# Dilated attention with its tokens tiled by parity: four blocks of 128 keys in every step of a two-layer decoder kernel

## What is computed

```
B_GROUPS = ((128, 1), (512, 4), (2048, 16))     # (window, dilation)
...
# Query t attends keys t, t-dil, ..., t-win (causal)
s = q . k * dh ** -0.5 + bias[bucket(distance)]
...
w = softmax over the groups of their lse
out = sum over the groups of w * o
```

## Time and profile before

| | |
|---|---|
| median of 3 runs | 798.08 us (796.19 to 800.15) |
| the profiled execution | 795.02 us, of which 793.0 us are the span |
| TensorE clock granted | 0.993 of full speed |
| TensorE busy | 97% of the span |
| VectorE, ScalarE, GpSimd busy | 68%, 58%, 29% |
| the attention blocks | 65.2 us each, from about 324 to 585 us |

### The profile page before, as it was taken

The page is one execution under the profiler, slowest core; times in us unless marked ns, Lnnn a source line. Parts: engine busy times, 40 slices in busy tenths (PEclk is TensorE's granted clock), DMA queues, the critical chain, the costliest instruction groups (busy, mean ns, idle before and its releaser), DMA issues.

```text
span 793.0 us, 17171 instructions
## 1 busy us (share of the span) xinstructions
PE 767.4 (97%) x6550; PEld 751.1 (95%) x6550; DVE 538.5 (68%) x983; ACT 462.4 (58%) x608; POOL 226.7 (29%) x190
## 2 busy tenths in 40 slices
PE   7999989999999999999999999999999999999995
PEld 7989889999999999999999999999899999999995
DVE  5776867887888546557646646655678888788442
ACT  6642657666565456358647737735856665655451
POOL 2520224333222532222222221201232234222331
PEclk9999999999999999999999999999999999999998
DMA  9653425665655555856586295475625756554721
GB/s 292 205 160 110 150 80 193 212 197 175 199 188 183 182 184 176 241 175 145 173 237 141 84 258 122 148 218 157 168 70 188 238 173 199 176 195 147 239 93 53
DMA packets 135613, 137.27 MB, mean 173 GB/s; under 512 B 3521, under 2 KB 134932, under 8 KB 135572
## 3 DMA queue, kind: packets, MB, share of 16 engines
q1 hardware_dynamic: 127808, 130.03, 50.4%
q10 hardware_dynamic: 7764, 6.67, 6.6%
HBM read 135.57 MB, written 1.12 MB: 172 GB/s over the span
## 4 chain that ended last, share of the span: by engine, by line
PE 53%; DVE 24%; issue 11%; ACT 7%; DMA 2%; DVEq 1%; ACTq 0%; POOL 0%; POOLq 0%
DVE wlo L845 9%; PE bank L1301 7%; PE bank L1303 6%; PE bank L1302 6%; PE banks L1301 6%; PE banks L1303 6%; PE banks L1302 6%; DVE cb L1090 3%; PE bank L1523 3%; PE banks L1590 2%; PE bank L1525 2%; DVE bank L1084 2%; ACT cb L671 2%; PE bank L1524 2%; PE banks L1555 2%
## 5 line engine op out<-in xcount | busy, mean ns | idle before, releaser
L453 POOL TENSOR_TENSOR wlo<-raw,whi 128x512 fp32r<-128x512 f32 (+1 forms) x169 | 218.2, 1324 | 530.4 <-ACT whi L494 530.4
L494 ACT ACTIVATE whi<-raw 128x2048 fp32r<-128x2048 f32 (+1 forms) x136 | 238.0, 1751 | 198.0 <-PE banks L1303 81.0
L845 DVE TENSOR_TENSOR wlo<-raw,whi 128x1024 fp32r<-128x1024 f32 x161 | 197.9, 1267 | 15.8 <-ACT whi L494 15.1
L1301 PE MATMUL bank<-xsA,whi 128*128 128x256 f32 x568 | 159.5, 281 | 3.6 <-DVE wlo L920 3.4
L1303 PE MATMUL bank<-xsA,wlo 128*128 128x256 f32 x568 | 157.7, 278 | 0.0
L1302 PE MATMUL bank<-xsA,whi 128*128 128x256 f32 x568 | 157.7, 278 | 0.0
L1301 PE MATMUL bank<-xsB,whi 128*128 128x256 f32 x480 | 134.3, 280 | 0.4 <-DVE cb L1094 0.3
L1303 PE MATMUL bank<-xsB,wlo 128*128 128x256 f32 x480 | 132.7, 276 | 0.0
L1302 PE MATMUL bank<-xsB,whi 128*128 128x256 f32 x480 | 132.6, 276 | 0.0
L1301 PEld LDWEIGHTS bank<-xsA,whi 128*128 128x128 f32 x568 | 107.4, 189 | 5.1 <-issue 4.1
L1302 PEld LDWEIGHTS bank<-xsA,whi 128*128 128x128 f32 x568 | 107.5, 189 | 0.1
(11 more groups left out here) (209 smaller groups left out, 1577.4 us busy)
## 6 DMA issues: line engine op xcount, KB each, us to landing
raw<-in_f_w_up SPq DMA_DIRECT2D x44, 1024.0 KB, 5.1
raw<-in_w_kv SPq DMA_DIRECT2D x24, 1024.0 KB, 7.6
raw<-in_f_w_down SPq DMA_DIRECT2D x16, 1024.0 KB, 5.2
raw<-in_b_w_q SPq DMA_DIRECT2D x12, 1024.0 KB, 5.3
raw<-in_a_w_in SPq DMA_DIRECT2D x10, 1024.0 KB, 5.8
raw<-in_f_w_down SPq DMA_DIRECT2D x8, 768.0 KB, 4.9
Bi<-bias_by_distance ACTq DMA_DIRECT2D x16, 384.0 KB, 7.7
raw<-in_a_w_out SPq DMA_DIRECT2D x4, 1024.0 KB, 5.2
```

Source lines behind the costliest of these rows:

```text
L453: o = g.tensor_tensor(wlo[s][:, ka:kb, :], raw[s][:, ka * CW:kb * CW] .rearrange("p (k c) -> p k c", c=CW), whi[s][:, ka:kb, :].bitcast(F3 ...
L494: o = a.activation(whi[s][:, k0:k1, :], raw[s][:, k0 * CW:k1 * CW] .rearrange("p (k c) -> p k c", c=CW), ACT.Copy)
L845: v.tensor_tensor(wlo[s][:, ka:kb, :], raw[s][:, ka * CW:kb * CW].rearrange("p (k c) -> p k c", c=CW), whi[s][:, ka:kb, :].bitcast(F32), A ...
L1301: t_.matmul(ps, hi_w, hi_x, start=first, stop=False)
```

## The change

Tokens go into two tiles by parity, the even ones and the odd ones. A group with dilation 4 or 16 then needs only the key tile of the query's own parity, and the group with dilation 1 needs both. Each step has four blocks of 128 keys: 512 wide, exactly one PSUM bank. The order of the tokens is changed where the input of the attention is made (`gained`, by `by_parity`, on ScalarE and VectorE in the last stage of layer 0) and changed back where a head's output is stored (`head_out`). The bias table has 5 rows of 256 for a head: group 0 for same parity, groups 1 and 2, and group 0 for the other parity twice, for the two directions. Scores rotate over banks 3 to 5, transposes alternate between banks 6 and 7.

```
-DIST = 384
+DIST = 512
+BB = 5
...
-    dist = 255 - np.arange(DIST)
+    m = np.arange(DIST // 2)
+    dist = np.concatenate([254 - 2 * m, 255 - 2 * m])
...
         def score_out(s):
-            w = NG * P * (1 + s // 2 % 2)
-            c = s % 2 * (768 if s // 2 % 2 else 512)
-            return s_ps[:, c:c + w]
+            return bank[3 + s % 3][:, :]
+        def turned_bank(s):
+            return bank[6 + s % 2][:, :]
...
+                if u == 8:
+                    sp.wait_ge(bt_copied, 1)
+                    for g in range(NG):
+                        sp.dma_start(bvd[:, 1 + g, :], bv[g * BH:(g + 1) * BH, 0:S])\
+                            .then_inc(bv_out, 16)
+                    sp.dma_start(bvd[:, 0, :], bv[0:BH, S:DIST]).then_inc(bv_out, 16)
+                    sp.dma_start(bvd[:, BB - 1, 0:S - 1], bv[0:BH, S + 1:DIST])\
+                        .then_inc(bv_out, 16)
...
-                    act.wait_ge(bt_copied, 1)
-                    act.dma_start(bvd.ap(), bv[:, :]).then_inc(bv_out, 16)
...
-                    src = bass.AP(bvd, (hb * HB + h) * DIST, [[1, P], [BH * DIST, NG], [1, S]])
+                    src = bass.AP(bvd, (hb * HB + h) * (BB * S), [[1, P], [S, BB], [1, P]])
...
-                        pe.wait_ge(smax_done, hb * 8 + 2 * t)
+                        pe.wait_ge(smax_done, hb * 8 + (2 * t - 1))
                     for g in range(NG):
                         for j in range(2):
                             rows = slice(j * DH, (j + 1) * DH)
-                            mm = t_.matmul(score_out(2 * t + j)[:, g * w:(g + 1) * w],
-                                           QT[rows, g, hp, tt * P:(tt + 1) * P],
-                                           KT[rows, g, hp, 0:w], start=True, stop=True)
+                            ps = score_out(2 * t + j).rearrange("p (b k) -> p b k", b=4)
+                            keys = KT[rows, g, hp, :].rearrange("p (b k) -> p b k", b=NT)
+                            if g == 0:
+                                ps = ps[:, 0:2, :] if tt else ps[:, 0:4:3, :]
+                            else:
+                                ps, keys = ps[:, g + tt, :], keys[:, tt, :]
+                            mm = t_.matmul(ps, QT[rows, g, hp, tt * P:(tt + 1) * P], keys,
+                                           start=True, stop=True)
...
-                    if s:
-                        pe.wait_ge(ptlo_done, hb * 8 + s)
-                    for b in range(NG * (1 + tt)):
-                        mm = t_.transpose(t_ps[:, b * P:(b + 1) * P],
+                    if s >= 2:
+                        pe.wait_ge(ptlo_done, hb * 8 + (s - 1))
+                    for b, to in enumerate((0, 3, 1, 2) if head_of(s)[1] else (0, 1, 2, 3)):
+                        mm = t_.transpose(turned_bank(s)[:, to * P:(to + 1) * P],
                                           SB[:, s % 2, b * P:(b + 1) * P], ident[:])
...
-                        for g in range(NG):
...
-                            for kt in range(NT):
-                                w = Vs[:, kt, g, h, :, :].rearrange("p a e -> p (a e)")
-                                for x in (PTh, PTl):
-                                    mm = t_.matmul(
-                                        pv_out(h, slice(0, P), last)[:, kt * P:S], w,
-                                        x[:, h, g, 2 * kt:2 + kt, :].rearrange("p b q -> p (b q)"),
...
+                        product(h, 0, 0, 0, slice(0, NT))
+                        for g in range(1, NG):
...
+                            for tt in range(NT):
+                                product(h, g, tt, g, slice(tt, tt + 1))
+                        mm = product(h, 3, 1, 0, slice(0, NT))
```

More of the change, by code:

```diff
@@ L61 @@
 FB = (2, 3, 0, 1)
[L62 removed]
+PV_BANK = (5, 4)
 V_A, V_KV, V_B, V_F0, V_F1, V_FIN, V_HN = range(0, 56, 8)
@@ L300, in own_rows, with pv_out, head_out, by_parity @@
             return slice((h % 2) * DH, (h % 2 + 1) * DH)
-        def pv_out(h, rows, last):
-            return bank[PV_BANK[last][h // 2]][rows, (h % 2) * S:(h % 2 + 1) * S]
-        def head_out(hb, h, part, last):
+        def pv_out(h, rows):
+            return bank[PV_BANK[h // 2]][rows, (h % 2) * S:(h % 2 + 1) * S]
+        def head_out(hb, h, part):
             rows = own_rows(h)
             dst = aTs[rows, bass.ds(hb * 2 + h // 2, 1), part, :]\
-                .rearrange("p a (b t) -> p (a b) t", b=NT)
-            src = pv_out(h, rows, last).rearrange("p (b t) -> p b t", b=NT)[:, :, ::-1]
+                .rearrange("p a (j c) -> p (a c) j", c=2)
+            src = pv_out(h, rows).rearrange("p (c j) -> p c j", c=2)[:, :, ::-1]
             return dst, src
+        def by_parity(ap):
+            return ap.rearrange("p a (j c) -> p (a c) j", c=2)
+        def in_parts(ap):
+            return ap.rearrange("p a (c j) -> p (a c) j", c=2)
         def n_v(n):
@@ L1210, in a_sum @@
                     dve.wait_ge(cross_done, hb * HB + (h // 2 * 2 + 2))
-                    ps = pv_out(h, own_rows(h), last)
+                    ps = pv_out(h, own_rows(h))
                     v.tensor_tensor(ps, ps, cross[own_rows(h), :], ALU.add).then_inc(asum_done, 1)
@@ L1347, in sums @@
                 pe.wait_ge(acc_done, 8 * (s + 1))
-                mm = t_.matmul(bank[b][:, 0:S], ones[:], acc[:, :], start=True, stop=True)
+                ac = acc[:, :].rearrange("p (j c) -> p c j" if s == 2 else "p (c j) -> p c j", c=NT)
+                mm = t_.matmul(bank[b][:, 0:S], ones[:], ac if s == 2 else acc[:, :], start=True,
+                               stop=True)
                 if tokens:
                     for tt in range(NT):
-                        mm = t_.matmul(bank[b][:, S + tt:S + tt + 1], acc[:, tt * P:(tt + 1) * P],
+                        mm = t_.matmul(bank[b][:, S + tt:S + tt + 1], ac[:, tt, :],
                                        ones[:, 0:1], start=True, stop=True)
@@ L1580, in mixed, with product @@
                         pe.wait_ge(ev_done, hb * 18 + (E_QKV + 18))
-                        if not last:
-                            pe.wait_ge(smax_done, hb * 8 + 8)
+                        pe.wait_ge(smax_done, hb * 8 + 6)
+                    def product(h, b, kt, g, q):
+                        w = Vs[:, kt, g, h, :, :].rearrange("p a e -> p (a e)")
+                        for x in (PTh, PTl):
+                            mm = t_.matmul(pv_out(h, slice(0, P))[:, q.start * P:q.stop * P], w,
+                                           x[:, h, b, q, :].rearrange("p b q -> p (b q)"),
+                                           start=b == 0 and x is PTh,
+                                           stop=b == 3 and x is PTl)
+                        return mm
                     for h in (2 * c, 2 * c + 1):
-                        for g in range(NG):
+                        product(h, 0, 0, 0, slice(0, NT))
+                        for g in range(1, NG):
                             if midway and (h, g) == (1, 1):
                                 midway()
-                            for kt in range(NT):
-                                w = Vs[:, kt, g, h, :, :].rearrange("p a e -> p (a e)")
-                                for x in (PTh, PTl):
-                                    mm = t_.matmul(
-                                        pv_out(h, slice(0, P), last)[:, kt * P:S], w,
-                                        x[:, h, g, 2 * kt:2 + kt, :].rearrange("p b q -> p (b q)"),
-                                        start=g == kt == 0 and x is PTh,
-                                        stop=g == NG - 1 and kt == 1 and x is PTl)
+                            for tt in range(NT):
+                                product(h, g, tt, g, slice(tt, tt + 1))
+                        mm = product(h, 3, 1, 0, slice(0, NT))
                     mm.then_inc(pv_done, 1)
```

71 lines of the change are left out of this document (31 added, 40 removed).

## The result

| | before | after |
|---|---|---|
| median | 799.12 us (796.19 to 800.71, 4 runs) | 790.77 us (789.53 to 791.79, 4 runs) |
| the profiled execution, its span | 795.02, 793.0 us | 791.78, 789.7 us |
| one attention block, start to start | 65.23 us | 64.04 us |
| last block with its seam | 51.74 us | 49.14 us |
| bias load, issue to landing (least, median, most) | 5.8, 7.7, 12.7 us | 3.2, 4.6, 8.2 us |

The ratio is 0.9898 with a 95% interval of 0.9873 to 0.9924: faster by 1%. The profiled span fell by only 3.3 us, less than the 4.4 of the sum.

The account below looks back on a forecast made before the run. TensorE, with work for 97% of the span, was taken as the bound; -1.7 - 1.8 - 1.0 + 1.0 - 1.2 + 0.3 = -4.4 us, put on the 798.08 us median, gave 793.7 us, range 789.5 to 801.5.

Parts of the forecast that it names:

- Scores: Score products in the attention blocks: two wide and four narrow ones per step pair, 1.28 us a pair, -1.7 us in all.
- Transposes: Transposes on TensorE in the attention blocks: 4 + 4 instead of 3 + 6 a head, 16 fall away, -1.8 us.
- Products with the values: Attention matmuls with the values: fewer columns but still 12 a head, paced by weight loads and not width, 0 us.
- Step 2: Attention blocks: the 0.24 us wait of the transposes' weight load for the softmax goes, -1.0 us in four blocks.
- step 0: Start of each attention block: a longer softmax chain adds a TensorE wait of 0.21 to 0.35 us, +1.0 us in four blocks.
- Last block: Last attention block, no projection tile between steps: weight-load waits of 0.85, 0.80 and 0.71 us shrink, -1.2 us.
- Small edits: Layer 0's bias table: wider float32 products and a longer copy out of PSUM, +0.3 us; other edits about 0.
- Layer 0 as a whole: Beyond the small edits nothing was priced in layer 0; a change above 1 us would show the prediction wrong.
- TensorE's own work: Scores and transposes on TensorE: their work falls by 3.5 us, otherwise the prediction would be wrong.
- Profile to median: Whole kernel: the -4.4 us sum takes the profiled 795.02 to 790.6 us; the median, 3 us higher, goes to 793.7.
- Rival 1: Bias loads in the attention blocks: more pieces at a fixed cost land late, 15 us lost, 808.7 us; chance 0.10.
- Rival 2: Attention blocks: bias loads 1.4 us longer, or a doubled step 0 wait, give back 1 to 3.5 us; 796.5 us, chance 0.20.

## Why the prediction was right, and where it was not

- **Scores** -1.7: right. A group costs 1.28 us, as worked out, eight times 0.21.
- **Transposes** -1.8: right, 0.45 us for four.
- **Products with the values** 0: right in its reason (the wide products), a little short in size. 0.08 us per 24, about 0.6 in four blocks, are gained. With all of them wide, in the new order, it is the same 2.83 us, so it isn't the columns. Whether it is the order or the fewer changes from narrow to wide, no run tells. What the prediction found to agree within 7 ns is the pace; a single weight load shows as 0.19 us in the trace and overlaps the next.
- **Step 2** -1.0 and **step 0** +1.0: right. The 0.24 us wait is gone and the new one is 0.28, though only in two blocks (0.15 and 0.11 in the others). Moving `turned(0)` takes it away again, 0.85 us in all.
- **Last block** -1.2: the right waits shrank, somewhat more than priced. Step 6 has 0.29 left of 0.85, step 7 nothing that is marked of 0.80 (0.3 was forecast), and the low part 0.60 of 0.71: 1.5 us. A wait of 0.38 at step 5, which the sum did not have, is still 0.31.
- Together the blocks were to gain 4.7 us and gained 6.2. The products (0.6), the last block (0.3) and the smaller step 0 (0.2) make 1.1 of the 1.5; the rest I can't place.
- **Small edits** +0.3: right for what it prices. The table costs 0.3 us by the second profiles and 0.6 by the first, and TensorE's wait at 43 us grew from 1.48 (1.37 in the second) to 1.65. The copy takes 0.68 instead of 0.54 us.
- **Layer 0 as a whole** is the step that failed. The sum has nothing there beyond these edits, and the sentence "I would be wrong if layer 0 changed by more than 1 us" came true: up to the first block 2.87 us were lost, 2.37 of them in the output projection, 1.37 by the clock and about 1 us by VectorE behind GpSimd. Neither belongs to the new layout: the run with the rows apart has the layout and neither of the two. Nor does the place in the span decide, since that run resumes latest of all. As far as the profiles show, both come and go with the execution, and I had priced only what the edits add.
- **TensorE's own work** was to fall by 3.5 us. Start to start it did (scores and transposes). The busy time of the page fell by 1.6 us in the first profiles, 3.5 in the second, and 4.9 against the run with only the copy moved, in which the clock doesn't fall here, so that sum is no measure of it.
- **Profile to median.** The sum was put on the median unchanged. The profiled execution of before was a quick one of a wide scatter, that of after one of the longer kind. I had no row for either. That the time came out inside the range is in part luck: the blocks gained 1.5 us more than the sum, the output projection lost 2.4 that it did not have, and 2.4 to 5 us of the fall of the median are no term of it.
- **Rival 1** did not happen, but its place was well chosen: with the rows apart it takes 23 us. My two readings of the earlier trace rows (cost by piece or by byte) were both wrong. The Trainium skill's count of transactions ("DMA: Bandwidth & Descriptors", section How a descriptor splits into AXI transactions) has no change from before to after. The median landing fell from 7.7 to 4.6 us, and with the same pieces it goes to 9.5, so the count is not the price here.
- **Rival 2** has nothing for it: the loads came earlier, not later.

Still open: what makes the clock fall behind one wait of 2.3 us and not behind another, what sets GpSimd's start against VectorE's, what spreads the old kernel with its rows together over the 2.3 us that are left, and why the median fell by 2.4 to 5 us more than the profiles differ.

## What to carry to other kernels

In a stream that one engine fills, count its instructions by start to start and the few waits by their chains. Most of those terms came out within a few tenths. Then ask of every stretch that the change doesn't touch whether its executions differ among themselves, and take more than one profile before a difference there is put down to an edit: the copy of a small table, moved off the path, came out 3.8 us quicker in its one execution, of which some 0.75 are its own. When many pieces are read again and again from DRAM, lay out side by side what one load reads before counting pieces or bytes.

## What the runs showed of the hardware

- The same wait of 2.3 to 2.4 us is followed by 1.2 GHz or not. In six profiles (the changed kernel twice, all products wide, step 0 later, one bank, smaller pieces) the stream resumed at 105.40 to 105.58 us after it, and in all six the clock fell (0.79 in 104 to 112 us). In five it did not fall: four resumed between 104.73 and 105.24 us (the kernel before, again, with its rows together, and the copy moved), and one at 105.77 (rows apart). So neither the layout nor the place in the span decides, and what does is not shown. With work in the gap (8 or 12 products, three profiles) it stayed at 2.4 GHz. A fall costs 1.37 us here.
- Loads whose pieces come from rows 16 or 24 KB apart take 9.5 and 7.7 us in the median; from rows side by side 4.6 us, whether in 640 pieces of 512 B or 384 of 1 KB.
- A VectorE operation with two SBUF inputs goes from 0.47 to as much as 1.5 us beside a GpSimd one, and one with a PSUM input doesn't change (0.41).
